# A two-layer hybrid decoder on one core: 64 bytes of padding between the weights' slots, the gathered tokens' rows and the turned activations' rows

## What is computed

```python
def swiglu(x, w_gate, w_up, w_down):
    return (jax.nn.silu(x @ w_gate) * (x @ w_up)) @ w_down

def moe_swiglu(x, w_router, w_gate, w_up, w_down):
    ...
    for e in range(N_EXPERTS):                       # 8 experts, hidden width 3584
        out = out + combine[:, e:e + 1] * swiglu(t, w_gate[e], w_up[e], w_down[e])

for l in range(DEPTH):                               # DEPTH = 2
    mix = token_mixer(h, w_in[l], ...)
    h = layer_norm(ALPHA * h + mix, ln1_g[l], ln1_b[l])
    f = swiglu(h, ...) if l % 2 == 0 else moe_swiglu(h, ...)
    h = layer_norm(ALPHA * h + f, ln2_g[l], ln2_b[l])
```

## The kernel before, in words

| tensor | start before | pitch of slots or rows before | start modulo 256 | start after | pitch after | start modulo 256 after |
|---|---|---|---|---|---|---|
| w_hi | 53376 | 8192 | 128 | 53376 | 8256 | 128 |
| w_lo | 77952 | 8192 | 128 | 78144 | 8256 | 64 |
| hT_hi | 115584 | 1088 | 128 | 115968 | 1088 | 0 |
| hT_lo | 124288 | 1088 | 128 | 124672 | 1088 | 0 |
| xg_hi | 166464 | 512 | 64 | 166848 | 576 | 192 |
| xg_lo | 174656 | 512 | 64 | 176064 | 576 | 192 |
| ag_hi | 186944 | 512 | 64 | 189376 | 576 | 192 |
| ag_lo | 188992 | 512 | 64 | 191680 | 576 | 192 |
| y_hi, y_lo, ST | 191040, 195136, 165440 | | 64 each | 193984, 198080, 165824 | | 192 each |

## Time and profile before

### The profile page before, as it was taken

How to read it: one execution, slowest core, us unless ns; L and a number is a source line. 1 busy time by engine, 2 the same in 40 slices (tenths; PEclk the granted TensorE clock), 3 DMA queues, 4 the chain that set the end, 5 groups by cost and what they waited for, 6 DMA issues and landing times.

```text
span 1871.6 us, 28531 instructions
## 1 busy us (share of the span) xinstructions
PE 1836.2 (98%) x11042; PEld 1629.6 (87%) x11042; DVE 1389.8 (74%) x1167; ACT 1101.1 (59%) x857; POOL 36.7 (2%) x77
## 2 busy tenths in 40 slices
PE   8999999999999999999999999999999999999996
PEld 8999999999999999997888888888888888888885
DVE  4755666654556566667888889888898888888987
ACT  5534254534345443456777776776777777777774
POOL 0200100000001101000000000000000000000000
PEclk9999999999999999998999999999999999999998
DMA  8625524444535455354999989999989999999993
GB/s 330 205 91 185 178 104 184 155 158 155 182 125 202 147 185 200 113 184 156 365 368 356 364 341 349 370 364 369 346 335 370 362 357 362 336 355 362 362 365 132
DMA packets 72897, 492.76 MB, mean 263 GB/s; under 512 B 9120, under 2 KB 9888, under 8 KB 14944
## 3 DMA queue, kind: packets, MB, share of 16 engines
q1 hardware_dynamic: 68720, 482.44, 69.1%
q0 software_dynamic: 2480, 5.64, 1.1%
q10 hardware_dynamic: 1600, 3.31, 0.6%
HBM read 483.66 MB, written 1.05 MB: 259 GB/s over the span
## 4 chain that ended last, share of the span: by engine, by line
PE 58%; DVE 1%; issue 1%; ACT 0%; DVEq 0%; ACTq 0%
PE ps L712 12%; PE ps L714 12%; PE ps L713 12%; PE ps L1023 6%; PE ps L1026 5%; PE ps L1025 5%; PE ps L1006 1%; PE ps L1044 1%; PE ps L1065 0%; PE ps L1066 0%; PE ps L967 0%; PE ps L958 0%; PE ps L866 0%; PE ps L870 0%; PE ps L1053 0%
## 5 line engine op out<-in xcount | busy, mean ns | idle before, releaser
L1752 DVE TENSOR_TENSOR w_lo<-raw,w_hi 128x2048 fp32r<-128x2048 f32 x336 | 763.1, 2289 | 124.2 <-ACT w_hi L1171 121.8
L1171 ACT ACTIVATE w_hi<-raw 128x2048 fp32r<-128x2048 f32 x336 | 637.8, 1918 | 179.9 <-PE ps L1026 97.4
L423 DVE TENSOR_TENSOR w_lo<-raw,w_hi 128x2048 fp32r<-128x2048 f32 (+2 forms) x130 | 277.5, 2142 | 188.7 <-ACT w_hi L416 187.4
L712 PE MATMUL ps<-hT_hi,w_lo 128*128 128x272 f32 (+1 forms) x1392 | 402.4, 289 | 12.5 <-DVE w_lo L423 8.4
L714 PE MATMUL ps<-hT_hi,w_hi 128*128 128x272 f32 (+1 forms) x1392 | 400.9, 288 | 0.0
L713 PE MATMUL ps<-hT_lo,w_hi 128*128 128x272 f32 (+1 forms) x1392 | 400.8, 288 | 0.0
L712 PE MATMUL ps<-w_hi,xg_lo 128*128 128x512 f32 x896 | 357.3, 399 | 1.7 <-DVE xg_lo L2141 1.7
L714 PE MATMUL ps<-w_hi,xg_hi 128*128 128x512 f32 x896 | 351.3, 392 | 0.0
L713 PE MATMUL ps<-w_lo,xg_hi 128*128 128x512 f32 x896 | 350.4, 391 | 0.0
L416 ACT ACTIVATE w_hi<-raw 128x2048 fp32r<-128x2048 f32 (+2 forms) x132 | 234.5, 1782 | 189.4 <-PE ps L714 141.8
L712 PEld LDWEIGHTS ps<-hT_hi,w_lo 128*128 128x128 f32 x1392 | 264.1, 190 | 15.1 <-DVE w_lo L423 8.6
(11 more groups left out here) (285 smaller groups left out, 1857.4 us busy)
## 6 DMA issues: line engine op xcount, KB each, us to landing
raw<-in_dense_units SPq DMA_DIRECT2D x116, 1024.0 KB, 4.9
raw<-in_moe_w_gate SPq DMA_DIRECT2D x112, 1024.0 KB, 6.9
raw<-in_moe_w_up SPq DMA_DIRECT2D x112, 1024.0 KB, 7.0
raw<-in_moe_w_down SPq DMA_DIRECT2D x112, 1024.0 KB, 7.0
raw<-in_dense_units SPq DMA_DIRECT2D x8, 512.0 KB, 4.0
v_tok<-turned_v POOLq DMA_DIRECT2D x48, 64.0 KB, 2.3
raw<-in_dense_units SPq DMA_DIRECT2D x8, 256.0 KB, 6.1
srT<-o_tok ACTq DMA_DIRECT2D x6, 272.0 KB, 4.3
```

Of the source, the lines that this page charges most:

```text
L423: nc.vector.tensor_tensor(w_lo[:, u % HALVES, 0:k * n], raw[:, u % RAW, 0:k * n], w_hi[:, u % HALVES, 0:k * n].bitcast(F32), ALU.subtract) ...
L712: nc.tensor.matmul(dst, l_lo, r_hi, start=start, stop=False)
L1171: return nc.scalar.activation(dst, src, ACT.Copy, **kw)
L1752: tt(w_lo[:, at % HALVES, :], raw[:, at % RAW, :], w_hi[:, at % HALVES, :].bitcast(F32), ALU.subtract).then_inc(lo_ready, 1)
```

## The change

Each of the six tensors is declared 16 float32 (64 bytes) longer in its last dimension, and used without those 16 columns. So the slots of `w_hi` and `w_lo` are 8256 bytes apart, the rows of `xg_hi`, `xg_lo`, `ag_hi` and `ag_lo` 576. All that is declared later moves up. `raw` stays as it is. No instruction is added, removed or moved on any engine, and no wait; the only thing that reads differently is the shape of the instructions that write `xg` and `ag`: four blocks of 128 columns with a gap where there were 512 in one piece.

```diff
+STEP = 16
...
-        w_hi = sb(ctx, "w_hi", [P, HALVES, UNIT], F32R)
-        w_lo = sb(ctx, "w_lo", [P, HALVES, UNIT], F32R)
+        w_hi = sb(ctx, "w_hi", [P, HALVES, UNIT + STEP], F32R)[:, :, 0:UNIT]
+        w_lo = sb(ctx, "w_lo", [P, HALVES, UNIT + STEP], F32R)[:, :, 0:UNIT]
...
-        xg_hi = sb(moe, "xg_hi", [P, 2, KT, P], F32R)
-        xg_lo = sb(moe, "xg_lo", [P, 2, KT, P], F32R)
+        xg_hi = sb(moe, "xg_hi", [P, 2, KT, P + STEP], F32R)[:, :, :, 0:P]
+        xg_lo = sb(moe, "xg_lo", [P, 2, KT, P + STEP], F32R)[:, :, :, 0:P]
...
-        ag_hi = sb(moe, "ag_hi", [P, 4, P], F32R)
-        ag_lo = sb(moe, "ag_lo", [P, 4, P], F32R)
+        ag_hi = sb(moe, "ag_hi", [P, 4, P + STEP], F32R)[:, :, 0:P]
+        ag_lo = sb(moe, "ag_lo", [P, 4, P + STEP], F32R)[:, :, 0:P]
```

## The result

The changed kernel takes 1877.72 us (median of 18 runs, 1874.56 to 1881.95) against 1871.2 us before (18 runs, 1869.61 to 1874.48): a ratio of 1.0034, 95% interval 1.0025 to 1.0042, which is 6.4 us slower (4.7 to 7.9). The forecast was 1868.6 us, with 1860 to 1876 as the range and 0.14 for slower. The profiled execution took 1881.95 us. Executions of one and the same kernel spread with their mean granted clock (after: 1874.56 us at 0.992, 1881.95 us at 0.989; before: 1869.61 to 1874.48), so that the spans of the two profiled executions, 8.5 us apart, can't be subtracted, and only stretches at the full clock are compared.

The account below looks back on a forecast made before the run. TensorE's own rate was taken as the bound; 1.8 us less in gate and up plus 0.9 in down, all else 0, made 2.7 us less, 1868.6 us against 1871.33, with an 80% range of 1860 to 1876.

Parts of the forecast that it names:

- What bounds the kernel: Both stages: TensorE sets the time by its own rate; only the distance between matmuls can move it.
- Part (2): Experts' gate and up, 2688 matmuls: stream distance modulo 256 bytes turns evenly through four 64-byte steps, 1.8 us less.
- Part (3): Experts' down product, 1344 matmuls: half at stream distance 0, a quarter each at 64 and 192 bytes, 0.9 us less.
- Part (1): Dense stage: a quarter of the matmuls at each stream distance both before and after, cost 0.
- Parts (4) to (6): Scatter's matmuls keep their stream distance; four-block `xg` and `ag` writes and ScalarE's and VectorE's new slot addresses: 0 each.
- phase 1 is the good phase: Experts' 512-column matmuls: leaving stream distance 64 costs 2.1 ns each, 6.3 us more, 1877.6 us; chance 0.13.
- The large gain: Experts' 512-column matmuls: standing still at one stream distance is dear, turning saves 14.3 us, 1857 us; chance 0.24.
- The phase means nothing: Experts' 512-column matmuls: stream distance modulo 256 bytes has no effect, time stays 1871.3 us; chance 0.16.

Follow-up runs that it names:

- w_lo_turned: Kernel before plus only a 64-byte gap between `w_hi` and `w_lo`, no padding: 1879.45 us against 1870.71, ratio 1.0043.
- w_only: Kernel before with only the padding of `w_hi` and `w_lo`, rows of `xg` and `ag` unpadded: 1875.84 us against 1869.99, ratio 1.0032.
- slots_alike: Kernel before with padded `w_hi` and `w_lo` slots, a gap putting `w_lo` back in line with `w_hi`, `xg` and `ag` unpadded: 1876.28 us, ratio 1.0027.
- x_only: Kernel before with only the padding of `xg` and `ag`, weight slots unpadded: 1874.97 us, ratio 1.0028.
- phase_0: Kernel before plus a 64-byte gap ahead of the experts' tensors, no padding; their streams stand at distance 0: 1862.54 us against 1869.99, ratio 0.9962.
- phase_3: Kernel before plus a 128-byte gap ahead of the experts' tensors, no padding; their streams stand at distance 192: 1884.96 us against 1869.99, ratio 1.0078.

## Why the prediction was wrong, point by point

**What bounds the kernel: right.** The distance between matmuls moved; the other engines stayed, and no wait of TensorE grew in the experts.

**Part (2), gate and up: the failed step.** "I take the 256-column rows, because 512 columns are, like 256, a whole number of 256-byte turns." At 512 columns the units cost 2.72, 2.75, 2.79 and 2.80 us in phases 0 to 3. The rows turn evenly, as I said, which gives (2.72 + 2.75 + 2.79 + 2.80) / 4 = 2.765 us for 2.75: 224 x 0.015 = 3.4 us more, where I had 1.8 us less. The trace has 4.9 us more (the means of the four gate and up units of a chunk, 87 ns longer together, x 56).

**Part (3), down: the same step.** With my own shares (half in phase 0, a quarter each in 1 and 3) the 512-column prices give 2.7475 us, 0.3 us less in all; I had 0.9 less. The trace has 0.2 us less, but not for that reason: the second down unit went from 2.75 to 2.78 us, dearer like the rest, and the first one got shorter only because its late first matmul takes 0.24 us where it took 0.29 (medians).

**What the sum lacked in the experts.** 3.4 - 0.3 = 3.1 us of the 4.5 that the stretch grew by. The other 1.4 us lie in gate and up (4.9 us against 3.4). I priced each matmul by its own phase; in the change the phase moves on every third matmul and with `w_lo`, and the scatter shows that a move is paid for over several matmuls. `w_lo_turned` is the clearest case, 2.79 us where its own phases say 2.73. That these moves make up the whole 1.4 us is an argument, not a measurement, and a move isn't always dear: the down unit of `w_only` in slot 0 changes between phases 3 and 2 and takes 2.75 us, where its own phases say 2.80.

**Part (1), the dense stage at 0: wrong.** The argument, a quarter of the matmuls in each phase both times, is right where hi and lo lie alike (`slots_alike`, 72.24 us). With `w_lo` 64 bytes off it isn't, and the twelve units take 72.56 us. Kernels with before's dense addresses took 72.24 (`x_only`, phase_0) or 72.40 us (before). 0.16 to 0.32 us in 576 matmuls is 0.3 to 0.6 ns each. At 256 columns it went the other way; the 287 matmuls shown above for before, after:

```profile
790.69:824.37 33.68, 33.68 (x288) 1.00 0.41 148
```

Over the whole stage 272 columns take 125.92 ns for 125.48 (125.40 in phase_0), 256 columns 117.47 for 117.69 (117.66). On 4416 and 1440 matmuls, 5856 in all, that is 1.6 to 2.0 us more. With the experts' 4.5 it is 6.1 to 6.5 us, and the runs show 6.4.

**Parts (4) to (6): nothing in the profile against them.** VectorE's 2289 ns and the wait for `xg_lo`, 1.7 us, are as they were; that of the weight loads for `w_lo` fell to 7.1 us.

**The rivals.** The slow one, "phase 1 is the good phase", gave 1877.6 us, the time that came, and that is mostly luck: phases 2 and 3 are dearer, but phase 0 is cheaper, and part of the loss is in the dense stage, which it didn't touch. Its price came from the scatter, in phase 0 and dear (231.3 ns), the one row at 512 columns. That row was misread, by the prediction and by the rival alike: the same eight matmuls in the same phase take 226.7 ns each in phase_0, so 231.3 was the price of coming out of phase 1, not that of phase 0. The large gain fell with everything else: to stand still in one phase is not dear as such, since phase 0, which stands still, is the cheapest of all and phase 3, which stands still too, the dearest. "The phase means nothing" fell with phase_0 and phase_3.

**The rule of the Trainium skill** ("SBUF — State Buffer", section "Who interferes with whom": independent ports for the moving operand and for LDWEIGHTS, and TensorE never waits) would have made all these kernels equal; the same instructions took 1862.5 to 1885 us by the distance of the two streams alone. What the streams share is not shown by any run. The page also says that DMA never contends with a compute engine, and there the traces agree: units of phase_0 take 2.72 us at a DMA share of 0.82 and of 1.02.

**What stays open.** Why the order turns with the number of columns, and the rule by which a matmul pays for its neighbours, with `w_only`'s cheap slot 0 among what it must explain. Also why one dense layout has two lengths, 72.24 and 72.40 us, in different executions.

## What to carry to other kernels

Where TensorE is the bound and each float32r matmul has its own weight load, the distance modulo 256 bytes between the moving row and the next stationary tile was worth 3% of a matmul here, for nothing but a gap in front of a tensor. At 512 columns, keep it constant from matmul to matmul and keep high and low halves alike (in the dense stage, at 272 columns, 128 bytes between them were a little cheaper), and sweep the few gaps on the chip at the kernel's own number of columns: phase 3 is the cheap one at 256 and the dearest at 512. A price read from rows of another shape is a reason to measure, not a forecast. Here the gap of 64 bytes with no padding (phase_0) beats both kernels, 1862.54 us.

## What was not expected of the hardware

- The distance between 512-column matmuls is 226.7, 229, 232.5 or 233.3 ns, by the distance of their streams in steps of 64 bytes, at a granted clock of 1.00 in each of these stretches. In cycles of 2.4 GHz the ends are 544 and 560: 32 and 48 over the 512 columns. At 256 columns the units shown have 120.0 and 113.8 ns, 288 and 273 cycles: 32 and 17 over.
- 32 bytes off distance 0 cost the full 16 cycles at 512 columns, on either side.
- The price of a distance is reached only some matmuls after the distance has changed: eight matmuls at distance 0 took 1.81 us behind matmuls at distance 0, 1.83 us behind distance 192, and 1.82 to 1.85 us behind distance 64.
- A typical unit's length repeats to 0.01 us, with the DMA engines at 0.8 or at 1.0 of their time; moving all operands together by 64 bytes changes none of them.
